# Token-major products with 512 weight columns per matmul, one PSUM bank each

## What is computed

```python
# first block
x = x + merged @ w_out[l]
h2 = rmsnorm(x, norm2_g[l])
x = x + jnp.square(jax.nn.relu(h2 @ w_up[l])) @ w_down[l]
# second block, for each of two layers
x = x + 0.5 * rms_norm(swiglu(rms_norm(x, ng[0]), ffn_w_gu[l, 0], ffn_w_down[l, 0]), ng[1])
mix = jnp.concatenate([tok, mem_out], axis=-1) @ w_o[l]
x = x + rms_norm(mix, ng[3])
x = x + 0.5 * rms_norm(swiglu(rms_norm(x, ng[4]), ffn_w_gu[l, 1], ffn_w_down[l, 1]), ng[5])
```

## Time and profile before

| what | value |
|---|---|
| median of three runs | 1473.21 us (1472.47 to 1478.81) |
| span of the profiled execution, first to last instruction | 1470.6 us |
| TensorE busy, matmuls | 1401.7 us, 95% of the span |
| VectorE, ScalarE, GpSimd busy | 922.4, 732.0, 192.7 us |
| weight transfers | 244.33 MB in all, mean 166 GB/s |
| mean granted TensorE clock | 0.982 of full |

### The profile page before, as it was taken

One profiled execution on the slowest core, in us unless ns is written; L12 is line 12 of the kernel. 1 busy time (PEld: TensorE's weight loads), 2 busy tenths in 40 slices (PEclk: granted clock), 3 DMA queues, 4 the chain that ended last, 5 costly groups with the idle time before them and its releaser, 6 DMA issues.

```text
span 1470.6 us, 28247 instructions
## 1 busy us (share of the span) xinstructions
PE 1401.7 (95%) x11538; PEld 1358.3 (92%) x11538; DVE 922.4 (63%) x1368; ACT 732.0 (50%) x1205; POOL 192.7 (13%) x210
## 2 busy tenths in 40 slices
PE   5899899999999999999998999999999989899998
PEld 5878799999999999998898999999999987899998
DVE  7998786666535665556765665556564467565644
ACT  7712755544435454455446454455444364554443
POOL 0465000022000111013101111011110010111100
PEclk9899899999999999999999999999999989999999
DMA  9223324455554555544342555544555341345551
GB/s 372 105 103 116 127 86 174 159 204 185 194 185 160 177 195 191 195 173 155 135 144 99 190 197 189 198 172 172 188 198 199 146 170 58 109 178 195 192 200 58
DMA packets 36815, 244.33 MB, mean 166 GB/s; under 512 B 4208, under 2 KB 5360, under 8 KB 8816
## 3 DMA queue, kind: packets, MB, share of 16 engines
q1 hardware_dynamic: 34992, 238.17, 44.7%
q10 hardware_dynamic: 1728, 4.81, 0.9%
HBM read 241.67 MB, written 1.05 MB: 165 GB/s over the span
## 4 chain that ended last, share of the span: by engine, by line
PE 81%; DVE 9%; ACT 5%; issue 2%; POOL 2%; DMA 1%; SPq 0%; DVEq 0%; ACTq 0%; POOLq 0%
PE ps L1891 49%; PE ps L1931 26%; DVE wlo L1083 3%; PE ps L2114 1%; PE ps L2140 1%; ACT whi L592 1%; DVE alo L1478 1%; PE ps L2130 1%; DMA xtok<-in_xt 1%; POOL pr L1809 1%; POOL pr L1808 1%; PE ps L2019 1%; ACT junk L829 1%; DVE yr L1456 0%; ACT pP L782 0%
## 5 line engine op out<-in xcount | busy, mean ns | idle before, releaser
L1083 DVE TENSOR_TENSOR wlo<-raw,whi 128x1024 fp32r<-128x1024 f32 (+1 forms) x434 | 505.1, 1205 | 273.3 <-ACT whi L592 273.2
L1891 PE MATMUL ps<-ahi,whi 128*128 128x256 f32 x2112 | 599.5, 284 | 32.1 <-DVE wlo L1083 18.0
L592 ACT ACTIVATE whi<-raw 128x1024 fp32r<-128x1024 f32 (+1 forms) x434 | 427.2, 1032 | 368.8 <-PE ps L1931 188.1
L1891 PE MATMUL ps<-alo,whi 128*128 128x256 f32 x2112 | 595.4, 282 | 0.0
L1891 PE MATMUL ps<-ahi,wlo 128*128 128x256 f32 x2112 | 594.0, 281 | 0.0
L1891 PEld LDWEIGHTS ps<-ahi,whi 128*128 128x128 f32 x2112 | 403.1, 191 | 38.2 <-issue 23.5
L1891 PEld LDWEIGHTS ps<-alo,whi 128*128 128x128 f32 x2112 | 402.8, 191 | 0.7 <-issue 0.7
L1891 PEld LDWEIGHTS ps<-ahi,wlo 128*128 128x128 f32 x2112 | 401.9, 190 | 0.0
L1829 POOL TENSOR_TENSOR hlo<-fh,hhi 128x256 f32 (+3 forms) x104 | 86.1, 828 | 756.2 <-ACT hhi L899 545.5
L1538 DVE TENSOR_TENSOR fa<-ps,r 128x512 f32<-128x512 f32 x104 | 71.9, 692 | 171.1 <-PE ps L1891 170.9
L1931 PE MATMUL ps<-whi,hhi 128*128 128x256 f32 x960 | 149.1, 277 | 0.0
(11 more groups left out here) (350 smaller groups left out, 1362.9 us busy)
## 6 DMA issues: line engine op xcount, KB each, us to landing
raw<-in_w_gu SPq DMA_DIRECT2D x88, 1024.0 KB, 4.8
raw<-in_w_fd SPq DMA_DIRECT2D x44, 1024.0 KB, 4.8
raw<-in_w_up SPq DMA_DIRECT2D x16, 1024.0 KB, 4.8
raw<-in_w_dn SPq DMA_DIRECT2D x16, 1024.0 KB, 4.8
raw<-in_w_ret SPq DMA_DIRECT2D x13, 1024.0 KB, 4.8
raw<-in_w_mg SPq DMA_DIRECT2D x8, 1024.0 KB, 4.9
raw<-in_w_o SPq DMA_DIRECT2D x8, 1024.0 KB, 6.3
raw<-in_w_mem SPq DMA_DIRECT2D x4, 1024.0 KB, 4.7
```

What stands on the lines that cost most here:

```text
L592: nc.scalar.activation(whi[:, m % SPL, c], raw[:, n % RAW, c], ACT.Copy).then_inc(S("w_hi"), 1)
L1083: ins = tt(wlo[:, m % SPL, c], raw[:, n % RAW, c], whi[:, m % SPL, c].bitcast(F32), ALU.subtract)
L1891: ins = mm(dst, lhsT, rhs, start=k == 0 and p == 0, stop=k == kt - 1 and p == len(pairs) - 1)
```

## The change

In `down` the four pieces of 256 columns become two of 512. The output of one matmul is now a whole bank, `start` is set at the first matmul into each bank (before: at the first into its lower half alone), and `skip_group_check`, an argument for the builder, falls away. Operands, sums, their order over `k` and `p`, banks, waits and semaphore signals stay.

```diff
-                                for c in range(4):
-                                    ws = slice(kk * D + T * c, kk * D + T * c + T)
-                                    ins = mm(two(2 + 2 * t + c // 2)[:, c % 2], x[:, k, xs], wgt[:, n_slot(n), ws],
-                                             start=u + kk + p + c % 2 == 0, stop=u == n_units - 1 and kk == 1 and p == 2,
-                                             skip_group_check=True)
+                                for c in range(2):
+                                    ws = slice(kk * D + 2 * T * c, kk * D + 2 * T * c + 2 * T)
+                                    ins = mm(PS[2 + 2 * t + c][:, :], x[:, k, xs], wgt[:, n_slot(n), ws],
+                                             start=u + kk + p == 0, stop=u == n_units - 1 and kk == 1 and p == 2)
```

## The result

The changed kernel takes 1483.42 us (median of 17 runs, 1479.45 to 1488.28) against 1475.16 us for the kernel before, run beside it (17 runs, 1472.3 to 1480.97). The ratio is 1.0052, with a 95% interval of 1.0038 to 1.0067: slower by half a percent, some 8 us, where I had forecast 22.8 us faster. The profiled execution has a span of 1479.4 us, 8.8 above the one shown of before.

What follows compares the result with a forecast made beforehand. TensorE's matmuls times pitch bound the kernel; gains of 7.5 us in w_dn, 11.4 in w_fd, 1.9 in w_out, 1.5 and 0.5 in the w_o products sum to 22.8 us, giving 1450.4 us, range 1444 to 1463.

Steps and rivals of the forecast that it cites:

- What bounds the kernel: Whole kernel: TensorE, busy 95% of the span; its long unbroken product pieces take matmuls times pitch.
- The excess and who makes it: Narrow matmuls in `down`: 6.7 to 13.3 ns above their columns' 106.7, blamed on a weight load of about 110 ns.
- the first case: Trace's fp32 matmuls of 256 columns, 512 cycles, one weight load each: pitch 215.5 ns, taken as 216 for wide fp32r.
- the gap of N / 2.4 + 2.5 ns: The Trainium skill's warm back-to-back matmul spacing: agrees with the row at 512 columns, gives 109 ns at 256.
- The reading of the 24-column stream: Stream of 24-column matmuls, pitch 110 ns: a weight load of 128 columns needs about that however short its matmul.
- Rival 1: In `down`, the excess belongs to each matmul, so a pair saves one: 13.6 us, 1459.6 us; chance 0.30.
- two pipelines falling in step: w_dn against w_fd: differing pitches for same code and tiles look like this, not a fixed cost; argued against rival 1.
- The untouched streams: w_up at 113.7 ns and w_gu at 117.8 expected to stay; if moved, w_up loses 3.0 us, a w_gu wins 4.4.
- my 7.5 us for w_dn: Forecast gain in w_dn: 384 pairs at 235.6 - 216 = 19.6 ns each.
- Supply, transitions, flags, the first matmul of a stretch: In and around `down`: splits and transfers keep up, transitions run as before, flags and exposed first loads costed at nothing.
- The slower rival: In `down`, the load is exposed behind each wide matmul: 320 ns pitch, 148 us slower, 1621 us; chance 0.03.
- the rival of an unchanged pace per column: In `down`, operand reading sets the pitch per column, so no gain: 1473 us; chance 0.05.

Runs made afterwards that it cites:

- e1: The changed kernel with hhi and hlo moved by 192 bytes, level with whi and wlo modulo 256: 1475.12 us, ratio 1.0011 to the kernel before.
- e2: The kernel before, with hhi and hlo moved by 192 bytes, level with whi and wlo modulo 256: 1489.86 us, ratio 1.0125.
- b1: The kernel before, unchanged, profiled again: w_up 84.80 us in place of 81.84, w_dn 87.06 in place of 90.46, second w_fd 62.20 in place of 59.87.
- e4: The kernel before, with ahi and alo moved by 128 bytes and hhi kept at 192 modulo 256: 1469.98 us, ratio 0.9963.
- e5: The changed kernel with hhi and hlo level with whi and wlo, and ahi and alo moved by 128 bytes: 1458.56 us, ratio 0.9905.

## Why the prediction was wrong

**What bounds the kernel** was right: TensorE's long pieces, matmuls times pitch, before and after.

**The excess and who makes it.** The failing step is "I take 216 ns as the pitch of a 512-wide fp32r matmul, for its columns and its load are those of the first case". The first case was of fp32 type. Equal array time and an equal load do not make an equal pitch: alone on TensorE, with 512 cycles of columns, fp32 has 215.8 ns, bf16 215.8, fp32r 226.7 to 234. The same goes for the gap of N / 2.4 + 2.5 ns. The row that I checked it against for 512 columns was an fp32 matmul of 256 columns and 512 cycles; bf16 has that gap at both widths (109.2 and 215.8 ns), fp32r at neither. The reading of the 24-column stream was sound as far as it went, since fp32r has 111.6 ns at 128 and 192 columns, but the conclusion that a load hidden behind wide columns takes the excess with it was only argued. The same sum with the measured 233.3 ns gives +6.5 ns per pair for w_fd, 6.9 us, and -2.3 for w_dn, -0.9 us; with w_dn's usual 113.3 ns of before it gives +2.5 us there. For the first w_o, 64 pairs x 13.3 ns are 0.85 us, as measured (0.8), in place of my 1.5.

**Rival 1** named the right place, "the excess belongs to the matmul, not to the load", and was mis-sized. I gave each wide matmul the excess of one narrow one, 6.7 to 13.3 ns. It was 20.0 in w_fd, w_dn and w_out and 13.3 in the first w_o (mhi, distance 0, 226.7 ns in its dense part). I took the smallest value seen at 256 columns as a floor for 512; but that value, 6.7 ns, belongs to a distance, and at that distance the wide form does badly. At distance 0 the rival's 13.3 ns per pair is what e1 against e2 shows: 1440 pairs, 19 us by the pieces, 15 by the medians.

**The hint I misread.** The trace of before had three pitches for one instruction form, and I put them down to two pipelines falling in step. That was half of it: 113.3 against 117.8 for the same code changes from one execution to the next, as b1 shows. But the 120 of the first w_o was not chance. It was the one token-major product with its tiles level, and the line `(64 - w[0]) % 128`, which places hhi, stood in the kernel to be asked about.

**The untouched streams.** "I expect these to stay" held for the four w_gu and failed for w_up, whose two pitches I had listed, at the price that I had given: 3.0 us. Both kernels show either pitch. Nor did I see that the pitches of w_up and w_dn are tied, so that my 7.5 us for w_dn rested on one execution.

**Supply, transitions, flags, the first matmul of a stretch:** all as said, at no cost that the trace shows. The slower rival, a load exposed behind each wide matmul (320 ns), and the rival of an unchanged pace per column (no gain) did not come true as mechanisms. The second came nearest in time, and by luck: with a fixed pace per column, 512 columns in w_fd would have stayed at 226.8 ns, where they went to 233.3, and level tiles would have stayed at e2's 240.0, where e1 has 226.8. Still it was right in one thing that I had dismissed: the placement runs tie the excess to where the two operands lie. To "slower" I gave 0.03, for a mechanism that isn't here. The range ended at 1463 because I let the excess per wide matmul be at most that of a narrow one. Its upper bound should have been the excess per column that was seen, 13.3 ns per 256 columns, 26.7 for 512: a pitch of 240, and a time on the slow side.

## What to carry to other kernels

Before a matmul is made wider or narrower, take its pitch from a stream of the same type, the same width and the same placement; if the trace has none, measure one, for a stream of 24 matmuls on TensorE alone costs 6 us. With fp32r operands the distance of the two start addresses modulo 256 bytes can be worth as much as the shape: of the distances tried in the kernel, 64 bytes was the best for 256 columns (113.3 or 117.8 ns) and 0 for 512 (226.7). And when one instruction form shows several pitches in one trace, sort them by address and profile the same program twice before reading anything into them.

## What the runs showed that I had not expected

- fp32r costs 6 to 16% over one column per cycle at full clock (113.3 to 123.3 ns at 256 columns, 226.7 to 234.4 at 512) where bf16 costs 1 to 2% (109.2 and 215.8).
- A 256-column fp32r stream at distance 64 runs at 113.3 or 117.8 ns, kept to its end, over up to 1008 matmuls (w_gu in e4 and e5), and both pitches were also seen with TensorE alone; w_up did so at distance 192 as well, where the four w_gu always had 117.8. This alone moves the same program's products by 2.3 to 3.4 us each from one execution to the next.
- A program's matmul of fp32 type stands in the trace as two MATMUL records with a weight load each: 24 in the program were 48 records, each 215.8 ns for 256 columns.
